# Retention and gated branch with 64 weight columns a product, and two moved waits

## The reference

```python
h = rmsnorm(x, norm_mix)
proj = h @ w_in                       # split into retention, gated (GLA), RWKV-7 and merge columns
y_ret, sr = retention_branch(...)     # 8 heads, keys 64, values 128
y_gla, sg = gla_branch(...)           # 4 heads, keys 128, values 256
y_rw, sw, ss = rwkv7_branch(...)      # 16 heads of 64
merged = gates[0] * (y_ret @ wb[0]) + gates[1] * (y_gla @ wb[1]) + gates[2] * (y_rw @ wb[2])
x = x + merged @ w_out
h = rmsnorm(x, norm_ffn)
x = x + (swiglu(h) if l == 0 else moe_swiglu(h))   # dense; then the two best of 8 experts
```

## Time and profile before

| | |
|---|---|
| median of 3 runs | 2635.6 us (2632.66, 2635.60, 2635.73) |
| profiled execution | 2633.36 us, its span 2631.6 us |
| granted TensorE clock, mean | 0.998 |
| PE busy | 2566.8 us, 98% of the span |
| PEld busy | 2052.2 us, 78% |
| DVE busy | 846.5 us, 32% |
| ACT busy | 582.0 us, 22% |

### The profile page before, as it was taken

The page is one execution under the profiler, slowest core; times in us unless marked ns, Lnnn a source line. Parts: engine busy times, 40 slices in busy tenths (PEclk is TensorE's granted clock), DMA queues, the critical chain, the costliest instruction groups (busy, mean ns, idle before and its releaser), DMA issues. The chain is left out here.

```text
span 2631.6 us, 81901 instructions
## 1 busy us (share of the span) xinstructions
PE 2566.8 (98%) x36246; PEld 2052.2 (78%) x36246; DVE 846.5 (32%) x2403; ACT 582.0 (22%) x1747; POOL 0.2 (0%) x4
## 2 busy tenths in 40 slices
PE   8999999999999999999999999999999999999998
PEld 5777876666677777677777666667799999999997
DVE  2022665666511000202266566651311111111111
ACT  2222333333301000122233333331111111111111
POOL 0000000000000000000000000000000000000000
PEclk9999999999999999999999999999999999999999
DMA  6432442222343433342354222224599999999997
GB/s 220 120 122 108 156 155 87 79 76 81 100 138 128 136 130 128 119 131 86 115 177 151 93 79 81 73 90 142 218 371 395 371 367 395 385 368 379 393 363 280
DMA packets 145550, 499.16 MB, mean 190 GB/s; under 512 B 18737, under 2 KB 23473, under 8 KB 142801
## 3 DMA queue, kind: packets, MB, share of 16 engines
q1 hardware_dynamic: 145360, 496.43, 53.1%
HBM read 476.07 MB, written 20.29 MB: 189 GB/s over the span
## 5 line engine op out<-in xcount | busy, mean ns | idle before, releaser
L315 PE MATMUL psum<-hT,ring 128*128 128x288 f32 x1788 | 477.8, 411 | 0.0
L408 PE MATMUL psum<-work,ring 128*64 128x88 f32 x11264 | 435.9, 239 | 4.6 <-issue 4.6
L408 PEld LDWEIGHTS psum<-work,ring 128*64 128x64 f32 x11264 | 433.5, 136 | 7.9 <-issue 7.5
L315 PEld LDWEIGHTS psum<-hT,ring 128*128 128x128 f32 x1788 | 323.5, 190 | 81.1 <-issue 3.1
L2169 PE MATMUL psum<-work,proj 128*64 128x88 f32 x5632 | 223.5, 239 | 1.2 <-issue 1.2
L2169 PEld LDWEIGHTS psum<-work,proj 128*64 128x64 f32 x5632 | 218.2, 136 | 5.8 <-issue 5.8
L401 PE MATMUL psum<-hT,ring 128*128 128x288 f32 x768 | 187.1, 406 | 0.0
L1460 ACT ACTIVATE work<-psum 128x256 f32<-128x256 f32 (+4 forms) x320 | 104.0, 362 | 357.1 <-PE psum L1373 84.8
L401 PEld LDWEIGHTS psum<-hT,ring 128*128 128x128 f32 x768 | 145.8, 190 | 40.9 <-issue 0.8
L1885 PE MATMUL psum<-hT,ring 128*128 128x288 f32 x704 | 171.0, 406 | 1.7 <-DVE hT L1964 1.7
L1885 PEld LDWEIGHTS psum<-hT,ring 128*128 128x128 f32 x704 | 133.7, 190 | 39.0 <-issue 2.1
(11 more groups left out here) (449 smaller groups left out, 3076.8 us busy)
## 6 DMA issues: line engine op xcount, KB each, us to landing
ring<-w_ff_dram SPq DMA_DIRECT2D x420, 512.0 KB, 6.5
ring<-w_mix_dram SPq DMA_DIRECT2D x256, 512.0 KB, 3.7
proj<-w_ff_dram SPq DMA_DIRECT2D x128, 512.0 KB, 5.4
proj<-w_ff_dram SPq DMA_DIRECT2D x64, 384.0 KB, 5.6
work<-s_gla_dram SPq DMA_DIRECT2D x8, 1024.0 KB, 5.4
gla_s_out<-work SPq DMA_DIRECT2D x8, 1024.0 KB, 4.6
work<-s_ret_dram SPq DMA_DIRECT2D x8, 512.0 KB, 4.6
ret_s_out<-work SPq DMA_DIRECT2D x8, 512.0 KB, 3.0
```

What stands on the lines that cost most here:

```text
L315: mm = (in_halves if self.narrow else nc.tensor.matmul)(out, ring[:, s, k, :], rhs[:, k, :], start=(k == 0), stop=(k == KT - 1))
L408: mm = nc.tensor.matmul(out[64 * c:64 * c + 64], ring[:, s, k, 64 * c:64 * c + 64], rhs[:, k0 + k, :], start=(k0 + k == 0), stop=(k0 + k = ...
```

## The change

Three things. In retention and in the gated branch the dense products, the prompt's scores, the outputs from scores and from the middle state, the gated branch's prompt states, and the square sums are issued by `in_halves`. Transposes, the rotation's swap, sample scores, sample states and the state products of retention stay as they were. PE's wait for retention's middle state moves from ahead of the first output product to ahead of the product that reads it, with a semaphore increment (`settle`) behind the wait. In the recurrent branch the load of the table for logarithm and exponential moves from the end of `gates` to the beginning of `key_scale`.

```diff
@@ -499,7 +499,7 @@
-                gla(KT)
+                gla(KT, True)
...
-                        nc.tensor.matmul(B[h][:, c], heads_of(kr, h)[:, c],
-                                         heads_of(qr, h)[:, c], start=True, stop=True)
+                        in_halves(B[h][:, c], heads_of(kr, h)[:, c], heads_of(qr, h)[:, c], start=True, stop=True)
...
                 pe.wait_ge(sig("state"), (i + 1) * 16)
-                pe.wait_ge(sig("mid"), i + 1)
                 for h in range(2):
-                    nc.tensor.matmul(B[h][:, 0:128], vtok[:, 0, h, :], att[:, h, 0, :], start=True, stop=True)
-                    nc.tensor.matmul(B[h][:, SAMPLE], vtokS[0:NS, h, :], attS[0:NS, h, :], start=True, stop=False)
-                gla(2)
+                    in_halves(B[h][:, 0:128], vtok[:, 0, h, :], att[:, h, 0, :], start=True, stop=True)
+                    in_halves(B[h][:, SAMPLE], vtokS[0:NS, h, :], attS[0:NS, h, :], start=True, stop=False)
+                gla(2, True)
...
-                gla(2)
+                gla(2, True)
                 for h in range(2):
-                    nc.tensor.matmul(B[h][:, 128:256], vtok[:, 1, h, :], att[:, h, 1, :], start=True, stop=False)
+                    in_halves(B[h][:, 128:256], vtok[:, 1, h, :], att[:, h, 1, :], start=True, stop=False)
+                pe.wait_ge(sig("mid"), i + 1)
+                settle(pe)
                 for h in range(2):
-                    mm = nc.tensor.matmul(B[h][:, 128:256], heads_of(mid, h), heads_of(qd, h)[:, 0:128],
-                                          start=False, stop=True)
+                    mm = in_halves(B[h][:, 128:256], heads_of(mid, h), heads_of(qd, h)[:, 0:128], start=False, stop=True)
                 mm.then_inc(sig("o_ps"), 1)
-                gla(4)
+                gla(4, True)
...
-                    mm = nc.tensor.matmul(B[2 + 3 * h][:, 0:T], ones, osq[:, h, :], start=True, stop=True)
+                    mm = in_halves(B[2 + 3 * h][:, 0:T], ones, osq[:, h, :], start=True, stop=True)
...
@@ -749,7 +748,7 @@
-                    last = mm(B[L % 2][:, c], kk[:, c], qq[:, c], start=True, stop=True)
+                    last = in_halves(B[L % 2][:, c], kk[:, c], qq[:, c], start=True, stop=True)
...
-                    last = mm(B[2][:, 0:T], ones, osq[:, h, :], start=(h == 0), stop=(h == 1))
+                    last = in_halves(B[2][:, 0:T], ones, osq[:, h, :], start=(h == 0), stop=(h == 1))
...
-                mm(ob[:, 0:128], vtok[:, 0, f], att[:, 0, :], start=True, stop=True)
-                mm(ob[:, SAMPLE], vtokS[0:NS, f], attS[0:NS, :], start=True, stop=False)
+                in_halves(ob[:, 0:128], vtok[:, 0, f], att[:, 0, :], start=True, stop=True)
+                in_halves(ob[:, SAMPLE], vtokS[0:NS, f], attS[0:NS, :], start=True, stop=False)
...
-                    rw(4)
+                    rw(4, True)
...
@@ -1476,9 +1475,9 @@
                     last = ac(gate[:, n, :], SIDE_BANK[n][:, 0:T], ACT.Sigmoid)
                 last.then_inc(sig("gates"), 1)
+
+            def key_scale(i):
                 nc.scalar.preload_act_table_set("natural_log_exp_and_others")
-
-            def key_scale(i):
                 act.wait_ge(sig("kk_ps"), i + 1)
```

More of the change, by code:

```diff
@@ L784, in prompt_states @@
                 pe.wait_ge(sig("ktok"), i + 1)
-                mm(B[5][:, 0:256], ktok[:, 0, :], vtok[:, 0, :], start=True, stop=True).then_inc(sig("mid_ps"), 1)
-                mm(B[3][:, 256:512], ktok[:, 1, :], vtok[:, 1, :], start=True, stop=True).then_inc(sig("fin_ps"), 1)
+                in_halves(B[5][:, 0:256], ktok[:, 0, :], vtok[:, 0, :], start=True, stop=True).then_inc(sig("mid_ps"), 1)
+                in_halves(B[3][:, 256:512], ktok[:, 1, :], vtok[:, 1, :], start=True, stop=True).then_inc(sig("fin_ps"), 1)
             def output(i, h):
@@ L801, in output @@
                            start=False, stop=(b == NB - 1))
-                mm(ob[:, 128:256], vtok[:, 1, f], att[:, 1, :], start=True, stop=False)
-                mm(ob[:, 128:256], mid[:, f], qb[:, 128:256], start=False, stop=True).then_inc(sig("o_ps"), 1)
+                in_halves(ob[:, 128:256], vtok[:, 1, f], att[:, 1, :], start=True, stop=False)
+                in_halves(ob[:, 128:256], mid[:, f], qb[:, 128:256], start=False, stop=True).then_inc(sig("o_ps"), 1)
             def sample_states(i):
@@ L828, in _ @@
                 output(i, 0)
-                rw(4)
+                rw(4, True)
                 output(i, 1)
-                rw(4)
+                rw(4, True)
                 sample_states(i)
-                rw(8)
+                rw(8, True)
             square_sum(GLA_H - 1)
```

## The result

| | before | after |
|---|---|---|
| median of 3 runs | 2635.6 us | 2618.8 us (2616.35, 2618.78, 2619.11) |
| profiled execution | 2633.36 us, span 2631.6 | 2616.35 us, span 2614.5 |
| granted TensorE clock, mean | 0.998 | 0.998 |

The ratio of after to before is 0.9941, 95% interval 0.9922 to 0.9961: the changed kernel is faster, by 16.8 us between the medians and 17.0 us between the two profiled executions. The prediction was 2615.5 us, in a range of 2610.5 to 2624.0.

What follows compares the result with a forecast made beforehand. TensorE, busy 98% of the span, was taken as the bound. Four terms, 8.1 + 4.4 + 2.9 + 2.8 = 18.2 us, took the profiled 2633.4 to 2615.2; the forecast was put at 2615.5 us, range 2610.5 to 2624.

Steps and rivals of the forecast that it cites:

- the signs that were to show it: No PE waits at L1275, first output or middle product; 0.2425 us passes; 0.4 and 0.9 us shorter stretches; expert stretch unchanged.
- the signs that were to show it wrong: A pass above 0.25 us, ACT waits at L1293 or L1313 and behind, or a wait at the middle product.
- Term 1: Recurrent branch: moving ACT's table load behind the copy of W removes PE's 0.58 us wait 14 times, 8.1 us.
- What is late next: Recurrent branch, PE 0.58 us earlier: ACT keeps 1.0 us; DVE's keys wait only if the reciprocal root passes about 529.4.
- Term 2: Retention's first output product: no longer waiting for the middle state saves 0.55 us, 8 times, 4.4 us.
- two bounds: Cost of `settle` after retention's moved wait: 0 or one change of shape, 0.095 us; 0 was taken.
- Term 3: Retention's shape changes: 1.09 us saved less 0.78 added, 0.31 a pair, 2.9 us in all with the first pairs.
- added side: Retention's new shape changes around the rotation's swap, value transposes and key transposes: 0.78 us a pair.
- d and s: Prices on PE: d, letting the array run empty, 0.095 us; s, loading 64 weight columns, 0.05 us.
- Term 4: Gated branch's shape changes: net 0.40 us saved a head, eight heads, less 0.4 at L838, 2.8 us.
- the likeliest case: Whole kernel: the forecast itself, chance 0.76, with the ends of its terms reaching from 2611 to 2619.5 us.

Runs made afterwards that it cites:

- Bonus product first: Changed kernel with DVE's query-key product for the bonus sum made ahead of the shift term; 2615.88 us, ratio 0.9924 to the kernel before.
- two groups wide: Changed kernel with the first two of a retention pair's six dense groups back at 128 weight columns; 2614.4 us, ratio 0.9925 to the kernel before.
- shapes only: Changed kernel with table load and middle wait put back, so only the 64-column products differ from the kernel before; 2629.6 us, ratio 0.9985.
- transposes together: Changed kernel with the gated branch's key transposes moved directly ahead of its value transposes; 2615.55 us, ratio 0.9928 to the kernel before.
- the kernel with all edits: Changed kernel plus bonus product first, two groups wide, transposes together, and L838's side products in halves; 2611.06 us, run again 2610.32 us.

## Why the prediction was right, and where its terms were off

The bound, the mechanism and the direction were right, and the signs that were to show it came, but for three sizes: 0.35 and 0.79 us a head and pair for 0.4 and 0.9, and an expert stretch 0.6 to 1.5 us shorter, which I take for scatter. None of the signs that were to show it wrong came: PE has no wait for ACT at L1293 or L1313, runs of halves between products of the same shape went at 0.2425 us a pass, and the middle product did not wait. What did come late was not among them: DVE's product for the bonus sum, just ahead of L1313. Term by term, predicted and measured in the branches:

| term | predicted | measured |
|---|---|---|
| 1, table load | 8.1 | 5.5 |
| 2 and 3, retention | 4.4 + 2.9 | 6.8 |
| 4, gated branch | 2.8 | 2.4 |
| rest | 0 | 2.3, scatter |
| span | 18.2 | 17.0 |

**Term 1** is the mis-sized one. The wait removed was 0.575 us (predicted 0.58), and the clearance of ACT was as worked out. The step that failed is "What is late next": I asked it of ACT and of DVE's key chain at 529.98, which lies behind, and passed over the very next product of PE, the bonus sum. DVE's product for it ended at 528.33 in the trace of before and the sum began at 528.82: 0.49 us of slack, of which after shows 0.06 to be needed between the two, so 0.43 was to be had at this step where PE came 0.575 earlier. The products behind it lost 0.04 more. Kept were 0.395 us an iteration, 5.5 us in 14. The bounds that I had given, 4 and 8.1, hold it. Bonus product first shows it: with that wait away the iteration is 0.58 us shorter than before.

**Term 2** was 0.55 a pair and measured 0.51 alone; 0.03 of the difference is at the first output product. That `settle` costs nothing stood as my choice between two bounds, and the trace bears it out.

**Term 3** was predicted at 0.31 a pair and measures 0.275 on top of the middle wait. Its added side was right: two groups wide took 0.60 of the predicted 0.78 away again, by d and s alone. Its hidden condition was that term 2 holds: shapes only got 0.10. The text counted the change into L531 as saved without saying that a wait covered it before.

**Term 4** was 0.40 a head and measures 0.35. The transposes cost what they should, as far as transposes together tested it; each output saved 0.26 instead of 0.30: 0.10 at its first products, 0.08 at L800 and 0.08 at L802 and the product from the middle state behind it (L803).

**The total** came nearer than the terms because the rest of the after profile happened to be 2.3 us shorter. That is luck: on the terms alone the profiled execution would have been 2618.7. The range held the time either way. Its working has a slip that did no harm: the text lets the likeliest case reach from 2611 to 2619.5, but its own low ends, 4, 3.6, 0 and 0.5, add up to 8.1 us, so 2625.3, above even the stated range, and no term has an end that gives 2611. About 2619.5 is what term 1 at its low end gives alone.

## What to carry to other kernels

When a wait is taken from an engine that bounds the kernel, everything that it reads in the next few microseconds comes under test: list each product behind the wait with the time at which its operand is ready, and take from the gain whatever exceeds the least slack, the nearest consumer first. Price changes of weight shape from the trace and then group instructions of one shape, but count a change only where PE isn't waiting anyway. Where single stages repeat to hundredths and the rest of the run scatters by microseconds, compare stages, since five runs' medians hid a real 4.8 us here; and look at what a program stage waits for at its end, since a store that landed late there cost 3.1 us of the 5.0 that a layer had gained in the kernel with all edits.

## What the runs showed of the hardware

- Of 24 passes from the gated to the recurrent branch in the twelve profiles, PE was idle 1.2 to 1.4 us in 19, and its granted clock behind them was 1.00. Of the five longer ones, those of 1.94 and one of 2.8 us kept 1.00; another of 2.8 and the ones of 3.0 and 3.4 us were followed by 4 us with a mean of 0.57 to 0.59, so for most of that time the lower of the two levels, 1.2 GHz instead of 2.4, and the first iteration became 1.6 to 1.7 us longer. I had no part of the prediction for this.
- From the issue of the gated branch's last 1024 KB store to the first product of the next branch it was 6.1 us in after, 7.6 in bonus product first and 8.0 in layer 1 of the kernel with all edits (1447.64 to 1455.62), at the same place of the program. The five long passes are those in which a 16 KB instruction packet, which took 0.94 to 1.59 us, went through beside the last stores; one sixteenth of the small store's packets then ended 1.7 to 2.2 us behind the others. With two stores of half the size PE idled 1.36 us without such a packet and 1.94 with one, in the one profile there is.
- Two halves of 64 weight columns ran at the pace of one product of 128 in all lengths of run that were seen, down to 4 passes. What a change of shape costs did not depend on which neighbour was wide: 0.095 us and 0.05 or 0.10 for the first load gave 0.59 us a pair and 0.29 a head, and 0.60 and 0.30 were measured.
